# Spreading per-token and per-head factors over the partitions: transposes of a broadcast tile in place of matmuls with the identity

## The reference

```python
def rmsnorm(x, g):
    y = xf * lax.rsqrt(jnp.mean(xf * xf, axis=-1, keepdims=True) + EPS)
    return y * g

hx = modulate(rmsnorm(x, g_pre_mix), sh1, sc1)
o_gla = rmsnorm(o_f + o_b, g_head).reshape(...) * silu(og)
x = x + gt1 * rmsnorm(yx @ w_out, g_post_mix)
hx = modulate(rmsnorm(x, g_pre_ffn), sh2, sc2)
x = x + gt2 * rmsnorm(conv_ffn(hx, ...), g_post_ffn)
...
h = rmsnorm_2(x, attn_norm)      # second block
h = rmsnorm_2(x, ffn_norm)
```

## Time and profile before

| | |
|---|---|
| median of 3 runs | 1450.05 us (1447.16 to 1454.12) |
| span of the profiled execution, first to last instruction | 1442.1 us |
| TensorE matmul busy | 1376.0 us (95%) |
| VectorE / ScalarE / GpSimd busy | 894.5 / 398.1 / 838.7 us |
| mean granted TensorE clock | 0.981 |

### The profile page before, as it was taken

How to read it: one execution, slowest core, us unless ns; L and a number is a source line. 1 busy time by engine, 2 the same in 40 slices (tenths; PEclk the granted TensorE clock), 3 DMA queues, 4 the chain that set the end, 5 groups by cost and what they waited for, 6 DMA issues and landing times.

```text
span 1442.1 us, 19719 instructions
## 1 busy us (share of the span) xinstructions
PE 1376.0 (95%) x6923; PEld 1110.6 (77%) x6923; DVE 894.5 (62%) x1274; ACT 398.1 (28%) x757; POOL 838.7 (58%) x651
## 2 busy tenths in 40 slices
PE   6999899989799999999999999999799999999998
PEld 4677678877488888887877888667588888888887
DVE  5696587763766666673128789635766888886000
ACT  3442223332422222201013202345513333332000
POOL 1343434426466666677756776433367777777775
PEclk9999999989899999999999999999999999999999
DMA  9466222112033333354332333211133333333332
GB/s 354 151 197 210 57 58 60 59 45 74 15 101 102 93 96 102 88 163 139 98 95 73 89 95 88 68 58 45 43 89 88 102 96 93 102 90 93 92 93 84
DMA packets 224459, 142.05 MB, mean 99 GB/s; under 512 B 5611, under 2 KB 211088, under 8 KB 224400
## 3 DMA queue, kind: packets, MB, share of 16 engines
q1 hardware_dynamic: 221333, 136.45, 31.6%
q10 hardware_dynamic: 3067, 4.78, 1.0%
HBM read 139.12 MB, written 2.10 MB: 98 GB/s over the span
## 4 chain that ended last, share of the span: by engine, by line
PE 83%; DVE 9%; issue 4%; POOL 2%; ACT 2%; DMA 0%; POOLq 0%; SPq 0%; DVEq 0%; ACTq 0%
PE ps L554 25%; PE ps L555 24%; PE ps L556 24%; PE ps L852 2%; POOL w_lo L517 1%; DVE norm_acc L1707 1%; DVE ada_acc L1804 1%; PE ps L1095 1%; PE ps L1111 1%; PE ps L1124 1%; DVE SS L2009 1%; ACT h_hi L1205 1%; PE ps L640 1%; POOL w_hi L514 1%; DVE xT L2180 1%
## 5 line engine op out<-in xcount | busy, mean ns | idle before, releaser
L517 POOL TENSOR_TENSOR w_lo<-raw,w_hi 128x1024 fp32r<-128x1024 f32 x213 | 535.8, 2516 | 17.8
L554 PE MATMUL ps<-h_hi,w_hi 128*128 128x512 f32 x1064 | 425.2, 400 | 14.2 <-DVE h_lo L1728 8.5
L556 PE MATMUL ps<-h_hi,w_lo 128*128 128x512 f32 x1064 | 417.1, 392 | 0.0
L555 PE MATMUL ps<-h_lo,w_hi 128*128 128x512 f32 x1064 | 416.9, 392 | 0.0
L513 POOL TENSOR_TENSOR w_hi<-raw,cst 128x16 fp32r<-128x16 f32 x213 | 63.9, 300 | 556.0 <-PE ps L556 501.7
L554 PEld LDWEIGHTS ps<-h_hi,w_hi 128*128 128x128 f32 x1064 | 201.1, 189 | 67.1 <-issue 17.7
L556 PEld LDWEIGHTS ps<-h_hi,w_lo 128*128 128x128 f32 x1064 | 201.1, 189 | 43.1
L514 POOL TENSOR_SCALAR w_hi<-raw 128x1008 fp32r<-128x1008 f32 x213 | 233.4, 1096 | 0.0
L555 PEld LDWEIGHTS ps<-h_lo,w_hi 128*128 128x128 f32 x1064 | 201.4, 189 | 39.2
L2098 DVE SCALAR_TENSOR_TENSOR f_acc<-ps,par,f_acc 128x441 f32<-128x441 f32 (+2 forms) x176 | 122.3, 695 | 50.2 <-ACT f_acc L1205 27.9
L554 PE MATMUL ps<-f_hi,w_hi 128*128 128x512 f32 x352 | 138.3, 393 | 0.6 <-POOL w_lo L517 0.5
(11 more groups left out here) (301 smaller groups left out, 1943.5 us busy)
## 6 DMA issues: line engine op xcount, KB each, us to landing
raw<-in_w_up SPq DMA_DIRECT2D x88, 512.0 KB, 3.7
raw<-in_w_in SPq DMA_DIRECT2D x59, 512.0 KB, 3.8
raw<-in_w_down SPq DMA_DIRECT2D x32, 512.0 KB, 3.6
ada_first<-in_w_ada SPq DMA_DIRECT2D x8, 1024.0 KB, 10.2
raw<-in_w_out SPq DMA_DIRECT2D x16, 512.0 KB, 3.6
v_tok<-in_w_ada SPq DMA_DIRECT2D x14, 512.0 KB, 5.0
raw<-in_w_down SPq DMA_DIRECT2D x16, 384.0 KB, 3.3
ada<-in_w_ada SPq DMA_DIRECT2D x10, 512.0 KB, 4.7
```

The costliest lines, as they stand in the source:

```text
L517: pool.tensor_tensor(w_lo[:, slot % 2, :], raw[:, slot, :], w_hi[:, slot % 2, :].bitcast(F32), ALU.subtract).then_inc(S("lo_split"), 1)
L554: nc.tensor.matmul(dst, lhs_hi, rhs_hi, start=first, stop=False)
L555: nc.tensor.matmul(dst, lhs_hi, rhs_lo, start=False, stop=False)
L556: return nc.tensor.matmul(dst, lhs_lo, rhs_hi, start=False, stop=last)
```

## The change

Both spreads call the transpose in place of the matmul, with the same operands, the same destinations, the same waits and the same semaphore after the last one. Stationary is still the broadcast column, moving is still the identity. The shares of the second block's attention (`spread_shares`, line 1141, 64 output partitions) are left as they are.

```diff
@@ -628,8 +628,8 @@
             pe.wait_ge(S("norm_inverted"), SUMMED.index(k) + 1)
             for t in range(n // P):
-                mm = nc.tensor.matmul(ps[:, stat_bank(k), t * P:(t + 1) * P], token_rinv[:, k, t:t + 1].broadcast_to([P, P]),
-                                      const("ident", P), start=True, stop=True)
+                mm = nc.tensor.transpose(ps[:, stat_bank(k), t * P:(t + 1) * P], token_rinv[:, k, t:t + 1].broadcast_to([P, P]),
+                                         const("ident", P))
             mm.then_inc(S(done), 1)
@@ -881,8 +881,8 @@
             pe.wait_ge(S("o_inverted"), c + 1)
             for h in range(GH):
-                mm = nc.tensor.matmul(ps[:, 6, h * P:(h + 1) * P], head_rinv[:, c, h:h + 1].broadcast_to([P, P]),
-                                      const("ident", P), start=True, stop=True)
+                mm = nc.tensor.transpose(ps[:, 6, h * P:(h + 1) * P], head_rinv[:, c, h:h + 1].broadcast_to([P, P]),
+                                         const("ident", P))
             mm.then_inc(S("o_spread"), 1)
```

## The result

The changed kernel has a median of 1452.22 us (22 executions, 1448.45 to 1456.64), the kernel before beside it 1447.50 us (22 executions, 1443.89 to 1454.68). The ratio is 1.0024 with a 95% interval of 1.0013 to 1.0034. The ratio is not that of the two medians, which lie 4.7 us apart (1.0033); it stands for 3.5 us, and the means, 1452.4 and 1448.5 us, lie 3.8 us apart. The change makes the kernel 0.24% slower where 0.3% faster was forecast; 1452.22 us lies above the range. In the groups of executions further down two single ones, of 2702 and 2679 us, ran in a slower state and are left out of every figure.

The account below looks back on a forecast made before the run. TensorE's queue, 83% of the chain, was taken as the bound. Eight four-tile spreads 3.7, spread 1 0.23 and spread 0 0.55 sum to 4.5 us, from 1450.05 to 1445.6 us; range 1441.6 to 1449.9.

Parts of the forecast that it names:

- 0.58 us at spread 5: Dense stream at spread 5: distance between weight matmuls ahead and behind falls from 1.04 to 0.58 us with four transposes.
- The broadcast: Stationary column repeated with step 0, in the spreads: taken to cost a plain transpose's 0.11 us, though no row shows it.
- what of it reaches the end: Step from passes saved at all ten spreads to the kernel's end: 4.5 of 4.8 us arrive, GpSimd's splits start earlier.
- The forecast for spread 6: Four-tile spread at the second block's last norm, ahead of its FFN: saves 0.46 us at full clock.
- A: Rival: part of the saving is absorbed by a just-hidden wait, in first 100 us or attention; 1448.7 us; chance 0.14.
- the head spreads: Four head spreads, chunks 0 to 3, of four tiles each: 0.46 us saved at each.
- spread 0 alone: Spread 0, in a stretch at 1.2 GHz with DMA full: 0.55 us taken, between nothing and 0.86.
- Rival B: Clock drops to 1.2 GHz at spreads in dense work, 3.4 us each; two falls give 1452.4 us; chance 0.06.
- the 7.95 us between span and median: Whole kernel: the median stands 7.95 us above the profiled span, and the forecast keeps the same distance.
- rival D: Clock falls less, at low stretches behind spreads 0 and 4: 3.4 us more gain, 1442.2 us; chance 0.05.

Follow-up runs that it names:

- e5_only6: Kernel before with only spread 6 (the second block's last norm, ahead of its FFN) as transposes; ratio 1.0021 to the kernel before.
- e6_allbut6: Kernel before with nine spreads as transposes and spread 6 left a matmul; ratio 0.9989 to the kernel before.
- e10_shortlo: Changed kernel with `w_lo` of the sixth `w_up` unit of the second FFN made for 128 of 1024 columns only; ratio 1.0009 to the kernel before.
- e12_behind2: Changed kernel with two more transposes behind spread 6, after its semaphore, into a bank nobody reads; ratio 1.0000 to the kernel before.
- e7_twice6: Changed kernel with the transposes of spread 6 done twice into the same places, ahead of the semaphore; ratio 0.9996 to the kernel before.
- e8_behind6: Changed kernel with four more transposes behind spread 6, after its semaphore, into a bank nobody reads; ratio 0.9993 to the kernel before.
- e9_poollate: Changed kernel with two small GpSimd multiplications ahead of the split of the second FFN's sixth `w_up` unit; ratio 1.0002 to the kernel before.
- e14_only24: Kernel before with only spreads 2 and 4 as transposes, matmuls elsewhere; ratio 1.0006 to the kernel before.
- e15_only15: Kernel before with only spreads 1 and 5 as transposes, matmuls elsewhere; ratio 1.0011 to the kernel before.
- e13_alltwice: Changed kernel with every transpose of all ten spreads done twice, so as many passes as before; ratio 0.9992 to the kernel before.
- e3_allbut0: Kernel before with nine spreads as transposes and spread 0 left a matmul; ratio 1.0025 to the kernel before.
- e11_veclate: Kernel before with all spreads but spread 6 as transposes, plus four small VectorE copies ahead of the second FFN's loop; ratio 1.0032 to the kernel before.

## Why the prediction was wrong

**Right.** One float32 product is two passes and one transpose is one: the counts 22 and 16. A transpose of a repeated column costs what any other does: 0.58 us at spread 5, as worked out from the earlier trace rows. The broadcast, for which no row stood, needed no price of its own.

**The step that failed** is in what of it reaches the end: "Behind the others there is TensorE's own work. GpSimd's splits can't come late by it: they waited 201 times for TensorE, 501.7 us in all, so they start as much earlier as TensorE is done earlier". They do start earlier, by 0.45 us, and that is the loss. It was taken for granted that an earlier start can only help, with the order of the other engines as it was. Behind spread 6 a short GpSimd instruction was 0.16 us behind a VectorE tap and is now 0.06 us ahead of it; VectorE then meets `w_lo`, falls back by 4.7 us against the 10.9 us of a pair and stays there, and TensorE pays at the end of the loop. The forecast for spread 6 was a gain of 0.46 us; e5_only6 measured a loss of 3.1 us at the same clock, and e6_allbut6 to e10_shortlo and e12_behind2 showed the cause. No rival had it. A spoke of a wait that was just hidden, but looked for it in the first 100 us and in the attention, and gave it only the power to take a gain away.

**The sum was too large also without that.** The five kernels with the other nine spreads short and 349.3 to 349.6 us behind spread 6 (e6_allbut6, e7_twice6, e8_behind6, e9_poollate, e12_behind2) lie at 1446.3 to 1446.7 us at the same clock: 2.2 us gained on average, where 4.5 - 0.46 = 4.0 was forecast. The terms were taken at the full value of the passes saved; the head spreads brought 1.0 +- 0.3 of 1.8, spread 0 alone 0.0 +- 0.4 of 0.55. That the piece on the chain shrinks by its full 0.46 us at spread 5 is seen in the trace; where the rest is absorbed was not found. e14_only24 and e15_only15 should show 0.9 and 0.7 us with errors of 0.3, and show none.

**Rival B, the clock, was half right, by a wrong mechanism.** The forecast left the clock as it was and gave B a chance of 0.06. The mean granted clock is lower where the spreads are short: 0.9742 +- 0.0004 over 59 executions of those five kernels, 0.9729 over 22 of the changed kernel, 0.9760 before. But e13_alltwice, all transposes and none saved, keeps 0.9768. So it is not that transposes count less than matmuls. This is also what stood against the rule in the Trainium skill, "TensorE: Matmul & The Clock Gate", Part 4, that the fast clock does not engage for transposes: the earlier trace rows had shown it engage, and e13_alltwice shows that twice as many of them cost the clock nothing. Why fewer passes lower the clock stays open. A part of it in the changed kernel goes with the new wait: in the trace the clock is down right behind it,

```profile
1335.00:1345.00 10.00, 6.55 (x22) 4.91 (x22) 3.81 (x3) 0.63 (x1) 5.50 (x4) 0.83 0.18 52
```

which is (1 - 0.83) / 0.5 x 10 = 3.4 us at 0.50. The profiled executions of e3_allbut0 and e5_only6, which have the wait too, read 0.83 at the same place, none without the wait does, but that of e11_veclate reads 1.00 behind a wait as long (3.45 us). At half speed 3.4 us cost a busy engine 1.7 us, so that a part of the 4.1 us of distance is this fall: from the end of the wait to the last transpose the changed kernel takes 112.3 us and e11_veclate 110.6. The other falls stand at other places from one execution to the next, so that single traces don't show which are due to the change.

**The account of the changed kernel.** Its mean is 1452.4 us, 3.7 above the 1448.7 of before. Nine shorter spreads give -2.4 or so (e6_allbut6); the step from there to the changed kernel at the same clock is +3.5 (1449.8 - 1446.3), where the distances give 4.1 with the stretch of low clock in it; and the lower clock, 0.0031, is 3.1 x 0.81 = 2.5 us. -2.4 + 3.5 + 2.5 = 3.6. All three come from one fit and so must nearly add up; what they tell is the sizes. Against the forecast of -4.5 that is 8 us too slow: 4.0 at spread 6 (3.5 lost, 0.46 not gained), 1.6 at the other nine (2.4 of 4.0), and 2.5 by the clock, of which the cause is open.

**A smaller fault of the forecast** was its starting point. The profiled execution of before had a clock of 0.981 and a time of 1443.9 us, next to the fastest of 22 (the time is the span and 1.8 us), so the 7.95 us between span and median were mostly scatter of the clock and not a distance that every execution keeps. Of the 1454.9 - 1442.1 = 12.8 us between the two profiled spans, 13 x 0.81 = 10.5 are the clock's, 0.968 against 0.981; reading these two traces side by side overstates the loss three times. The forecast of the median was not hurt by it, as the same 7.95 us were put back. It was hurt by the median of three, 1450.05 us, where 22 executions have 1447.50; worked out from that, the whole range would lie 2.6 us lower. And rival D says that TensorE has little to do in the low stretch at spread 0; its row has it busy for 6.37 of 6.83 us. That holds for the stretch at spread 4 alone, 3.55 of 6.80 us.

## What to carry to other kernels

Before a saving is summed up, look in the trace for pairs of engines that start within a few tenths of a microsecond of each other at the head of the loop behind it, and have instructions that lengthen each other; there an earlier start can be a loss, and the price is not set by the size of the saving (here 0.46 us saved, 4.1 lost). If a saving loses time, give the same length back at the same place (or delay one of the two engines there): that tells in one run whether the instruction or the moment is to blame. And compare single traces by distances within one stage, and whole kernels only over many executions with the granted clock of each beside its time.

## What the runs showed of the hardware that was not expected

- The loop of the second FFN has two rhythms with the same program: 349.5 us from spread 6 to the end, or 353.6. Which one is settled at its first pair: a GpSimd instruction of 0.22 us starts 0.06 us ahead of a VectorE tap (353.6) or 0.16 us behind it (349.5), which decides what `f_lo` meets. A late VectorE gets back almost nothing: in e11_veclate the lag goes from 12.7 us at the third pair to 12.3 at the last.
- A copy of 128x2 elements on VectorE, four times, took 2.51 us when it fell into a GpSimd subtraction with two inputs of 128x1024 (0.4 us had been estimated; no run has the copies by themselves).
- The granted clock falls in one execution and not in another at the same place with the same work ahead. The same window in e6_allbut6,

```profile
779.00:789.00 10.00, 7.85 (x25) 6.29 (x24) 6.29 (x8) 5.68 (x14) 4.06 (x3) 0.66 0.36 105
```

and in e7_twice6, the two programs being the same up to spread 6:

```profile
779.00:789.00 10.00, 7.83 (x41) 6.31 (x41) 6.29 (x8) 5.74 (x15) 4.48 (x4) 1.00 0.37 107
```

TensorE's busy time is 7.85 and 7.83 us, the clock 0.66 and 1.00. That is (1 - 0.66) / 0.5 x 10 = 6.8 us at half speed, which cost a busy engine 3.4 us, nearly as much as the whole change did.
